# A transformer layer on one core: float32r value products, a scan for the stick-breaking sums, and selection rounds placed anew

## The reference

```python
# D: stick-breaking attention, strictly causal (key position < query position)
z = q @ k.T * 64 ** -0.5
log_keep = where(causal, log_sigmoid(-z), 0.0)
log_w = log_sigmoid(z) + cumsum(log_keep, reverse=True) - log_keep
o_d = where(causal, exp(log_w), 0.0) @ v
# B: chunked attention, relative bias; C: two-chunk window with sinks, k and v shared by two heads
o_b = softmax(q @ k.T / 8 + bias) @ v
o_c = softmax with a sink(q @ k.T / 8 + bias) @ v
# A: an indexer of four heads scores all admissible keys; each query keeps its 128 best keys
o_a = softmax over the kept keys(q @ k.T / 8 + bias) @ v
y = sum of sigmoid(gates_i) * (o_i @ w_branch_i)
```

## Time and profile before

| what | value |
|---|---|
| median of three executions | 887.14 us (887.03 to 889.59) |
| the profiled execution, its own time | 887.8 us |
| span from its first to its last instruction | 886.1 us |
| mean granted TensorE clock | 0.994 |
| busy: TensorE, VectorE, ScalarE, GpSimd | 862.6, 477.0, 340.0, 30.0 us |
| attention slots 9 to 27 | 116 to 412 us of the span |

### The profile page before, as it was taken

The page is one execution under the profiler, slowest core; times in us unless marked ns, Lnnn a source line. Parts: engine busy times, 40 slices in busy tenths (PEclk is TensorE's granted clock), DMA queues, the critical chain, the costliest instruction groups (busy, mean ns, idle before and its releaser), DMA issues.

```text
span 886.1 us, 10410 instructions
## 1 busy us (share of the span) xinstructions
PE 862.6 (97%) x4079; PEld 706.4 (80%) x4079; DVE 477.0 (54%) x770; ACT 340.0 (38%) x503; POOL 30.0 (3%) x84
## 2 busy tenths in 40 slices
PE   7999999999999999999999989999999999999995
PEld 4989887887778877777888768888888888888884
DVE  4254699895758649736273486644433443222227
ACT  4354357765535535542242452222222222211112
POOL 2500000000000000000000100000000000000001
PEclk8999999999999999999999999999999999999998
DMA  6541221211212112212226123322222232222202
GB/s 237 179 179 55 90 95 48 77 67 48 93 50 96 48 48 95 95 47 96 96 95 237 47 72 119 143 95 95 95 95 95 95 101 93 108 103 103 102 9 95
DMA packets 14152, 85.02 MB, mean 96 GB/s; under 512 B 1680, under 2 KB 1940, under 8 KB 5280
## 3 DMA queue, kind: packets, MB, share of 16 engines
q1 hardware_dynamic: 11952, 77.34, 24.2%
q0 software_dynamic: 2016, 6.86, 2.3%
q10 hardware_dynamic: 144, 0.26, 0.1%
HBM read 82.33 MB, written 2.13 MB: 95 GB/s over the span
## 4 chain that ended last, share of the span: by engine, by line
PE 88%; DVE 8%; ACT 2%; issue 1%; DMA 1%; POOL 0%; SPq 0%; DVEq 0%; POOLq 0%; ACTq 0%
PE bank L1041 59%; PE bank L1195 17%; PE bank L1166 4%; DVE w_lo L704 1%; PE bank L1140 1%; PE bank L1153 1%; PE bank L1065 1%; DVE sel L776 1%; PE bank L1123 1%; PE bank L1124 1%; DVE top L774 1%; PE bank L1253 1%; DMA xraw<-in_xT 1%; DVE resid L922 1%; DVE result L1008 1%
## 5 line engine op out<-in xcount | busy, mean ns | idle before, releaser
L704 DVE TENSOR_TENSOR w_lo<-raw,w_hi 128x2048 fp32r<-128x2048 f32 x69 | 158.2, 2292 | 210.8 <-ACT w_hi L470 188.2
L1041 PE MATMUL bank<-x_hi,w_hi 128*128 128x512 f32 x720 | 184.0, 394 | 2.4 <-DVE y L709 1.2
L1041 PE MATMUL bank<-x_lo,w_hi 128*128 128x512 f32 x720 | 178.2, 390 | 0.0
L1041 PE MATMUL bank<-x_hi,w_lo 128*128 128x512 f32 x720 | 177.9, 389 | 0.0
L1041 PEld LDWEIGHTS bank<-x_lo,w_hi 128*128 128x128 f32 x720 | 135.2, 188 | 28.6
L1041 PEld LDWEIGHTS bank<-x_hi,w_lo 128*128 128x128 f32 x720 | 135.1, 188 | 28.1
L1041 PEld LDWEIGHTS bank<-x_hi,w_hi 128*128 128x128 f32 x720 | 132.5, 188 | 31.1 <-issue 5.2
L470 ACT ACTIVATE w_hi<-raw 128x2048 fp32r<-128x2048 f32 x48 | 92.1, 1918 | 122.3 <-PE bank L1195 94.9
L1195 PE MATMUL bank<-w_hi,h_hi 128*128 128x512 f32 x176 | 56.8, 389 | 0.0
L1195 PE MATMUL bank<-w_hi,h_lo 128*128 128x512 f32 x176 | 56.8, 389 | 0.0
L1195 PE MATMUL bank<-w_lo,h_hi 128*128 128x512 f32 x176 | 56.7, 389 | 0.0
(11 more groups left out here) (218 smaller groups left out, 1044.4 us busy)
## 6 DMA issues: line engine op xcount, KB each, us to landing
raw<-in_stream SPq DMA_DIRECT2D x69, 1024.0 KB, 4.8
resid<-in_x POOLq DMA_DIRECT2D x1, 2048.0 KB, 8.2
xraw<-in_xT SPq DMA_DIRECT2D x3, 512.0 KB, 8.5
out<-result SPq DMA_DIRECT2D x3, 512.0 KB, 2.6
bias_b<-bias_vectors POOLq DMA_DIRECT2D x1, 1024.0 KB, 6.4
bias_a<-bias_vectors POOLq DMA_DIRECT2D x1, 1024.0 KB, 12.5
ln_g<-in_g POOLq DMA_DIRECT2D x2, 512.0 KB, 7.6
ln_b<-in_b POOLq DMA_DIRECT2D x2, 512.0 KB, 8.7
```

What stands on the lines that cost most here:

```text
L704: dve.tensor_tensor(w_lo[:, s, :], raw[:, s, :], w_hi[:, s, :].bitcast(f32), ALU.subtract).then_inc(lo_ready, 1)
L1041: ins = pe.matmul(dst, lhs[a](k), rhs[b](k), start=n == 0, stop=n == n_all - 1)
```

## The change

**Value products.** `probsT` becomes two float32r copies, `pT_hi` (ScalarE, from the bank) and `pT_lo` (VectorE, bank less `pT_hi`). v of a head becomes a stack of 128 columns: the rounded v in the first 64 (`value_high`, ScalarE), the rest in the other 64 (`value_low`, VectorE). A unit has 8 float32r products of 128 columns of weights in place of 4 float32 ones of 64. The two halves of obank must then be added: ScalarE copies the lower half, VectorE adds the upper one (`o_sum`), ScalarE copies `o_hi` from it and VectorE subtracts for `o_lo`.

**Stick-breaking.** The scores of D are laid out with queries on partitions, as in the other branches. ScalarE forms Relu and Abs of z, Exp(-abs), and Ln(1 + .); VectorE sums both along keys from the right by `tensor_tensor_scan` (four, one for each row block), subtracts from the scaled scores, and ScalarE takes Exp. `unit_stage2` of D is then the 10 transposes too. The masks `neg_tri` and `neg_all` go.

**Order.** `ROUNDS` has 8 in slots 7 and 8, 2 in 9 to 12, 4, 3, 3, 3 in 13 to 16, and 4, 4, 3 in 18 to 20. `PAUSE` is 9 in place of 6.

```diff
-ROUNDS = {t: 7 if t < 9 else 5 if t < 13 else 2 for t in range(7, 21) if t != 17}
+ROUNDS = {7: 8, 8: 8, 9: 2, 10: 2, 11: 2, 12: 2, 13: 4, 14: 3, 15: 3, 16: 3, 18: 4, 19: 4, 20: 3}
...
 # ScalarE, unit_stage1, kind D
                     d = d_before(n)
+                    if d:
+                        act.wait_ge(pv_done, pv_before(n))
                     for b in range(3):
...
-                        act.activation(probs[:, s], score[b][:, 0:w], ACT.Copy, scale=SCALE).then_inc(z_ready, 1)
+                        act.activation(probs[:, s], score[b][:, 0:w], ACT.Relu, scale=SCALE)
+                        step(act.activation(probsT[:, s], score[b][:, 0:w], ACT.Abs, scale=SCALE))
                     unit_out(before)
+                    step_wait()
                     for b in range(3):
                         s = slice(b * 512, b * 512 + bank_width("D", b))
-                        act.wait_ge(abs_ready, 3 * d + b + 1)
-                        step(act.activation(probsT[:, s], probsT[:, s], ACT.Exp))
+                        step(act.activation(probsT[:, s], probsT[:, s], ACT.Exp, scale=-1.0))
+                    unit_out_high(before)
...
                     for b in range(3):
                         s = slice(b * 512, b * 512 + bank_width("D", b))
-                        act.wait_ge(sp_ready, 3 * d + b + 1)
-                        act.activation(sp_hi[:, s], probs[:, s], ACT.Copy).then_inc(sp_hi_ready, 1)
+                        act.wait_ge(log_ready, 3 * d + b + 1)
+                        last = act.activation(probs[:, s], probs[:, s], ACT.Exp)
+                    last.then_inc(stick_ready, 1)
...
 # ScalarE, unit_out, and the two new helpers
+                act.activation(o_sum[kind][0:HEAD, :], obank[HEAD:P, :], ACT.Copy).then_inc(o_part_ready, 1)
+            def unit_out_high(n):
+                act.wait_ge(o_sum_ready, pv_before(n) + 1)
+                act.activation(o_hi[rows, O_BUF[kind], h // 2, :], o_sum[kind][rows, :], ACT.Copy).then_inc(o_hi_ready, 1)
+            def value_high(n):
+                act.activation(value_stack(n)[:, :, 0:HEAD], value_head(kind, h), ACT.Copy).then_inc(v_hi_ready, 1)
...
 # ScalarE, slot loop
                 stack_high(UNIT_AT.get(t + 1))
                 if now is not None:
+                    if UNITS[now][0] != "I":
+                        value_high(now)
                     unit_stage1(now, before)
                 else:
                     unit_out(before)
+                if now is None or UNITS[now][0] != "D":
+                    unit_out_high(before)
...
 # VectorE, new helpers
+                dve.wait_ge(o_part_ready, pv_before(n) + 1)
+                dve.tensor_tensor(o_sum[kind][rows, :], obank[0:HEAD, :], o_sum[kind][0:HEAD, :], ALU.add).then_inc(o_sum_ready, 1)
+            def unit_out_low(n):
                 dve.wait_ge(o_hi_ready, pv_before(n) + 1)
+                dve.tensor_tensor(o_lo[rows, O_BUF[kind], h // 2, :], o_sum[kind][rows, :],
...
+            def probs_low(n):
+                for b in range(banks_of(kind)):
+                    dve.wait_ge(pT_hi_ready, stage2_banks_before(n) + b + 1)
+                    dve.tensor_tensor(pT_lo[kind][:, s], score[b][:, 0:bank_width(kind, b)], pT_hi[:, s].bitcast(f32),
+                                      ALU.subtract).then_inc(probsT_ready, 1)
+            def value_low(n):
+                dve.wait_ge(v_hi_ready, pv_before(n) + 1)
+                dve.tensor_tensor(v[:, :, HEAD:P], value_head(kind, h), v[:, :, 0:HEAD].bitcast(f32),
+                                  ALU.subtract).then_inc(v_lo_ready, 1)
...
 # VectorE, softmax_unit
                 unit_out(before)
                 stack_low(n + 1 if UNIT_AT.get(UNITS[n][2] + 1) else None)
+                unit_out_low(before)
                 search(first_round, rounds)
...
 # VectorE, stick_unit
                 unit_out(before)
                 stack_low(n + 1)
+                for r in (3, 2, 0, 1):
+                    dve.wait_ge(soft_ready, 3 * d + b + 1)
+                    step(dve.tensor_tensor_scan(probsT[:, s][:, ::-1], probs[:, s][:, ::-1], probsT[:, s][:, ::-1], 0.0,
+                                                ALU.add, ALU.add))
+                step_wait()
                 for b in range(3):
+                    dve.scalar_tensor_tensor(probs[:, s], score[b][:, 0:w], SCALE, probsT[:, s], ALU.mult,
+                                             ALU.subtract).then_inc(log_ready, 1)
+                unit_out_low(before)
...
 # VectorE, slot loop: first in the slot, and after stick_unit or ahead of softmax_unit
+                if before is not None and UNITS[before][0] != "I":
+                    probs_low(before)
...
+                if kind is not None and kind != "I":
+                    value_low(now)
...
 # TensorE
-            PAUSE = 6
+            PAUSE = 9
...
                 if kind == "D":
-                    pe.wait_ge(sp_lo_ready, 3 * (d_before(n) + 1))
...
+                    pe.wait_ge(stick_ready, d_before(n) + 1)
+                else:
+                    pe.wait_ge(probs_ready, soft_before(n) + 1)
...
                 for kb in range(TOK):
                     b, col, q0, width = key_place(kind, kb)
-                    ins = pe.matmul(obank[rows, q0:q0 + width], value_head(kind, h, kb),
-                                    probsT[:, b * 512 + col:b * 512 + col + width],
-                                    start=kb == 0, stop=kb == TOK - 1, skip_group_check=True)
+                    for part in (pT_hi, pT_lo[kind]):
+                        ins = pe.matmul(obank[:, q0:q0 + width], v[:, kb, :], part[:, b * 512 + col:b * 512 + col + width],
+                                        start=kb == 0 and part is pT_hi, stop=kb == TOK - 1 and part is not pT_hi,
+                                        skip_group_check=True)
```

More of the change, by code:

```diff
@@ L185, in layer_program @@
     probsT = at("probsT", R + 78 * K, [P, 1280], f32)
+    pT_hi = at("pT_hi", R + 78 * K, [P, 1280], f32r)
+    pT_lo, v_odd, o_sum = {}, {}, {}
+    for kinds, first, summed in (("D", R + 88 * K, R + 95 * K), ("B", R + 28 * K, R + 46 * K), ("CA", R + 61 * K, R + 46 * K)):
+        for kind in kinds:
+            pT_lo[kind] = at(f"pT_lo_{kind}", first, [P, 1280], f32r)
+            v_odd[kind] = at(f"v_stack_{kind}1", first + 5 * K, [P, TOK, P], f32r)
+            o_sum[kind] = at(f"o_sum_{kind}", summed, [P, SEQ], f32)
     sel = at("sel", R + 83 * K, [P, 1280], f32)
@@ L309, in stack_rows, with value_head, value_stack @@
             return slice(row, row + HEAD), slice(HEAD - row, 2 * HEAD - row)
[L311 to L314, removed]
+        def value_head(kind, h):
+            first = HEAD * (h // 2 if kind == "C" else h)
+            return va[kind][:, :, first:first + HEAD]
+        def value_stack(n):
+            return v_odd[UNITS[n][0]] if n % 2 else v_even
         def bias_keys(kind, h, width):
@@ L557, in unit_stage2 @@
                     w = bank_width(kind, b)
[L558 to L563, removed]
+                    act.activation(pT_hi[:, b * 512:b * 512 + w], score[b][:, 0:w], ACT.Copy).then_inc(pT_hi_ready, 1)
             def unit_out(n):
@@ L572, in unit_out @@
                 act.wait_ge(pv_done, pv_before(n) + 1)
-                rows = slice(HEAD * (h % 2), HEAD * (h % 2 + 1))
-                act.activation(o_hi[rows, O_BUF[kind], h // 2, :], obank[rows, :], ACT.Copy).then_inc(o_hi_ready, 1)
+                if pv_before(n):
+                    act.wait_ge(o_lo_ready, pv_before(n))
+                act.activation(o_sum[kind][0:HEAD, :], obank[HEAD:P, :], ACT.Copy).then_inc(o_part_ready, 1)
+            def unit_out_high(n):
+                if n is None or UNITS[n][0] == "I":
+                    return
+                kind, h, _ = UNITS[n]
+                rows = slice(HEAD * (h % 2), HEAD * (h % 2 + 1))
+                act.wait_ge(o_sum_ready, pv_before(n) + 1)
+                act.activation(o_hi[rows, O_BUF[kind], h // 2, :], o_sum[kind][rows, :], ACT.Copy).then_inc(o_hi_ready, 1)
+            def value_high(n):
+                kind, h, _ = UNITS[n]
+                what = "cvw" if kind == "C" else kind.lower() + "v"
+                act.wait_ge(act_emptied, emptied_before("act", TILE0[slot_of(what) + 1]))
+                if pv_before(n) >= 2:
+                    act.wait_ge(pv_done, pv_before(n) - 1)
+                act.activation(value_stack(n)[:, :, 0:HEAD], value_head(kind, h), ACT.Copy).then_inc(v_hi_ready, 1)
             def stack_high(n):
@@ L602, in _ @@
                 before, now = UNIT_AT.get(t - 1), UNIT_AT.get(t)
[L603 to L606, removed]
                 if before is not None and UNITS[before][0] != "I":
@@ L1157, in unit_values @@
                 kind, h, _ = UNITS[n]
[L1158 to L1162 removed]
+                pe.wait_ge(v_lo_ready, pv_before(n) + 1)
+                if pv_before(n):
+                    pe.wait_ge(o_sum_ready, pv_before(n))
```

(5 more changed lines are left out.)

94 lines of the change are left out of this document (29 added, 65 removed).

## The result

The changed kernel takes 910.07 us (median of 4 runs, 908.47 to 910.79), the kernel before 887.28 (4 runs, 887.03 to 889.59): a ratio of 1.025, 95% interval 1.0236 to 1.0264, so it is **22.8 us slower**. The forecast was 905.6, in a range of 896 to 918. The profiled execution took 909.6 us by its own time, its span is 907.8.

What follows compares the result with a forecast made beforehand. The prediction took TensorE and VectorE both to be at the limit, with VectorE's longer list deciding slots 7 to 20. Slot losses less small gains summed to +18.5 us on the 887.1 median: 905.6 us, range 896 to 918.

Steps and rivals of the forecast that it cites:

- TensorE's list: All units: cheaper value products save 16.3 us and D's stage 2 some 6.8, together 23 us off TensorE's work.
- B slots: Slots 14 to 16: VectorE's probabilities end at 17.2 us, TensorE is done at 14.7 and waits; +4.3 us in all.
- D slots: Slots 10 to 13: a chain through ScalarE and VectorE's scans gives three of 19.2 us and one of 19.6; +5.3.
- The scan: VectorE's sums along keys in D: 1.6 us at one pass, 3.2 at two; the forecast took 3.2.
- Rival (a): The scan is one pass, so slots 7 to 13 lose 6.4 us less: 899 us; chance 0.16.
- Slots 17 and 18: A later gate product delays slot 18's start by 0.5 us; `value_low` and two more rounds add 2.6.
- slots 19 to 21: VectorE's longer list sets 19 and 20 at 17.4 and 16.6 us, TensorE sets 21 at 13.7; +4.0 in all.
- slots 22 and 23: Small losses: +0.4 us at slot 22, as for the start of slot 18, and +0.3 at slot 23.
- the end: Slot 27 gains 0.3 us and nothing after it is touched: -0.3.
- rival (b): TensorE's clock falls after new waits in slots 13 to 20, up to 3 us a slot; four falls: 917; chance 0.20.
- Slot 24: `probs_low` stands behind eight additions on VectorE, so the scores wait: 17.9 us against 17.1, +0.8.
- Rival (c): VectorE's additions fit its idle time, so all of TensorE's 23 us come out: 864 us; chance 0.08 for below 884.

Runs made afterwards that it cites:

- the order experiment: The changed kernel with the low half of the output moved behind the rounds, all passes left on VectorE: 905.86 us.
- the filler: The changed kernel with 16 to 56 idle TensorE products ahead of the wait for the probabilities in slots 10 to 17 and 19 to 21: 908.13 us.
- the last version: The changed kernel with half passes on GpSimd, idle TensorE products in slots 10 to 13, rounds and other VectorE work placed by the trace: 877.44 us.
- the version with rounds in the gap: The changed kernel with the rounds of slots 10 to 12 ahead of `o_sum`, where VectorE idled 4.4 us: 910.93 us.
- both versions with the full set of fillers: The changed kernel with idle TensorE products in slots 10 to 17 and 19 to 21: 908.13 us; with D1 to D3's rounds ahead of `o_sum` too: 906.23.
- the GpSimd version: The changed kernel with the low halves of q, k and v on GpSimd and the output's low half behind the rounds: 892.71 us.

## Why the prediction was right

The forecast of 905.6 was 4.5 us low, inside its 901 to 911. Its mechanism held: TensorE's list got shorter, VectorE's got longer, and VectorE's end set each slot from 10 to 20, in D's slots by way of ScalarE's last Exp.

**TensorE's list.** Value products of 1.2 us: measured 1.29 at full clock. Stage 2 of D is now the ten transposes, 1.31 at full clock for a forecast of 1.1. Both savings are real and both wait. Only where VectorE has no rounds does the shorter list show: slot 21 took 13.67 us (forecast 13.7), slots 25 and 26 14.59 (14.7).

**B slots.** Forecast 17.2, measured 17.28, 17.45 and 17.28. The step in slot 16, where the wait for `o_hi` takes the place of `stack_low`, is shown by the order experiment: without that wait the slot is 14.9.

**D slots.** Forecast 19.2 three times and 19.6, measured 19.35, 19.28, 19.36 and 19.23. Slots 11 and 12 came out by the forecast's own steps (`pT_lo` late, `o_sum` at 161.72, the scans at 164.56), and the filler did not move them. Slot 10 agrees by two errors: without the clock's fall it takes 18.16, so its list was reckoned 1 us too long and the fall put that back.

**The scan.** This was the unknown cost: 1.6 or 3.2 us, and I took 3.2. Measured 2.98 for 1280 columns, as this row of the timeline of VectorE in slot 11 of the kernel after shows, where three banks of an elementwise pass (`SCALAR_TENSOR_TENSOR`) take 1.62:

```profile
164.56 2.97 DVE L888 TENSOR_TENSOR_SCAN probsT<-probs,probsT 128x512 f32<-128x512 f32 x4
167.56 1.62 DVE L894 SCALAR_TENSOR_TENSOR probs<-bank,probsT 128x512 f32<-128x512 f32 x3
```

The Trainium skill, DVE: opcode table, instruction layouts, handler registers and perf-mode slots, section Datapath and trigger behaviour, says half throughput; the trace agrees, 1.8 times the elementwise pass, with the start of four instructions in it. Rival (a) is out.

**The terms that were too small.** Slots 17 and 18 cost 4.6 for 3.1, slots 19 to 21 4.9 for 4.0, slots 22 and 23 2.4 for 0.7, and the end 1.2 for -0.3. The first three fell short by 1.5, 0.9 and 1.7, 4.1 us together. The filler tells how much of this was rival (b), the clock, in the slots that have it: 1.3 in slots 17 and 18 and 0.6 in slot 20. In slots 22 and 23 it is 1.5, by the two executions compared above. That is 3.4 of the 4.1. So rival (b) happened in part. The clock fell at slots 10, 12, 13, 17, 20 and 23, but cost at most 1.5 us each in place of 3, since where VectorE is late anyway the slower TensorE hides behind it. Slot 24 was forecast at +0.8 and came out at -0.4, because slot 23 ended late: with the clock held in slot 23 it takes 3.0 us more. Slots 22 to 24 together cost 2.0 for a forecast of 1.5. All in all the filler was worth 2 us.

The end is explained by the traces. In slot 27 TensorE waited 0.5 us for a gate product and 0.4 for `pT_lo`, and the way from slot 27 to the first layer norm grew by 0.2 where -0.3 was forecast. The other 1.3 us are not of the change: the 48 products with which the feed-forward part begins, which no edit touches, took 12.8 us in place of 11.5, with a clock of 0.59 in their first 3.2 us. In the other versions' traces they take 11.5 to 14.0, and 12.8 in the kernel before with GpSimd's passes. So a difference of two traces holds such a piece, and the start that was earlier by 2.0 us, by chance. The slots up to 26, which hold neither, sum to 22.5 us for a forecast of 18.8.

**Rival (c)**, VectorE's additions in idle time, is the one that the last version brings about: the passes go to an idle engine and the rounds go where VectorE idles. It still stops at 877, far from 864, in large part since slots 10 to 12 stay at 17.5 to 17.8 through ScalarE's and VectorE's chain, where TensorE's own list is 14.9 by the forecast's sum.

The experiments missed more than the prediction: the two halves of the change were forecast at 898.5 and 899 and took 904.9 and 909.0. The parts don't add: the rounds alone cost 10.8 us over the kernel before on the same chip, rounds and scan 16.3, rounds and split values 20.5, and all of it 22.8. Each of them ends in the same wait.

## What to carry to other kernels

When two engines end a slot within 1 us of each other, a change that gives one a shorter list and the other a longer one is worth what the longer list costs; work out both lists of the slot before writing it. Look for the third engine: four passes per unit on an idle GpSimd, dear as they are there, turned 905.9 into 892.7. Then place work that can stand anywhere, such as the selection rounds, by the idle pieces in the trace, one slot at a time: that was worth another 10 us. In the kernel before, where TensorE is the bound, three of those four passes moved were worth 1.4.

## What the hardware showed

**The clock after short waits.** TensorE's granted clock fell to 1.2 GHz for some microseconds after waits of 2.1 us (slot 12 of the version with rounds in the gap, window 0.57), and held at 1.00 through waits of 2.4 to 2.8 ahead of slots 14 to 16. The length of the wait alone doesn't decide it, and neither does its place: the wait of 2.45 us ahead of slot 23 was followed by the lower clock in one execution and by the full one in another, and the 2.64 ahead of slot 16, at 1.00 in the kernel after, by 0.64 over 4 us in the version with the rounds in the gap. What does decide it is not shown. Cheap products in the bank that is written next anyway held the clock in every slot that had them, in both versions with the full set of fillers.

**GpSimd beside VectorE.** A 64x512 subtraction takes VectorE 0.69 us and GpSimd 1.28 when it runs alone. Side by side each can stop the other: VectorE's 128x4 sign change went from 0.17 to 0.87 us (L862 of the kernel after, L885 with GpSimd) and ended at 214.91, when GpSimd's second pass of that slot had ended at 214.88. And these rows of both engines, around slot 9 of the GpSimd version, show `w_lo` at 3.00 in place of 2.29, beside GpSimd's first pass, GpSimd's second at 3.23 beside `w_lo`, and the scans at 4.32 in place of 2.97:

```profile
119.49 1.30 POOL L438 TENSOR_TENSOR q_stack_D<-qk_d,q_stack_D 64x512 fp32r<-64x512 f32 x1 [5.61 <-ACT k_stack_D L635]
120.86 3.23 POOL L440 TENSOR_TENSOR k_low_D<-qk_d,k_stack_D 64x512 fp32r<-64x512 f32 x1
124.17 1.28 POOL L442 TENSOR_TENSOR k_low_D<-qk_d,k_stack_D 64x512 fp32r<-64x512 f32 x1
```

```profile
119.93 3.00 DVE L747 TENSOR_TENSOR w_lo<-raw,w_hi 128x2048 fp32r<-128x2048 f32 x1
124.47 4.32 DVE L911 TENSOR_TENSOR_SCAN probsT<-probs,probsT 128x512 f32<-128x512 f32 x4 [1.53 <-ACT probsT L563]
```

The Trainium skill, SBUF — State Buffer, section SBUF: two separate sides, says that a GpSimd operation and a VectorE operation with two inputs in SBUF, as `w_lo` and the scan are, need the same pair of ports, and that the one that starts first has it for its whole instruction while the other is blocked. The trace agrees within 0.2 us for the first two pairs: GpSimd's second pass ended at 124.09, 1.2 us behind the end of `w_lo` at 122.93, and takes 1.28 undisturbed; `w_lo` ended 2.1 us behind the end of GpSimd's first pass at 120.79, and takes 2.29. It paid off here because GpSimd's 5 us in a B slot delay VectorE by 0.7 and relieve it of 2.5.
